# Expert weights of a streaming encoder's mixture layer: six conditional loads of 2 MB a round in place of twelve of 1 MB

## What is computed

```python
def moe(x, w_router, b_router, w_exp_gate, w_exp_up, w_exp_down):
    logits = (x @ w_router).astype(jnp.float32) + b_router.astype(jnp.float32)
    scores = jax.nn.softmax(logits, axis=-1).reshape(N, N_GROUPS, EXPERTS_PER_GROUP)
    ...
    for e in range(N_EXPERTS):
        h = jax.nn.silu(x @ w_exp_gate[e]) * (x @ w_exp_up[e])
        y = y + gates[:, e:e + 1] * (h @ w_exp_down[e])
    return y
```

## Time and profile before

| | |
|---|---|
| median of three runs | 1642.64 us (1641.89 to 1647.93) |
| profiled execution, its own time | 1645.16 us |
| span of its trace, first to last instruction | 1643.3 us |
| mean granted TensorE clock | 0.955 |
| TensorE busy (share of the span) | 1448.0 us (88%) |
| VectorE, ScalarE busy | 583.0 us (35%), 275.2 us (17%) |
| moved by DMA | 324.71 MB (millions of bytes), 198 GB/s on average |
| issues of expert loads | 6 groups of 54, 1024.0 KB each |

### The profile page before, as it was taken

One profiled execution on the slowest core, in us unless ns is written; L12 is line 12 of the kernel. 1 busy time (PEld: TensorE's weight loads), 2 busy tenths in 40 slices (PEclk: granted clock), 3 DMA queues, 4 the chain that ended last, 5 costly groups with the idle time before them and its releaser, 6 DMA issues.

```text
span 1643.3 us, 21243 instructions
## 1 busy us (share of the span) xinstructions
PE 1448.0 (88%) x6922; PEld 746.0 (45%) x6922; DVE 583.0 (35%) x1173; ACT 275.2 (17%) x671; POOL 90.4 (5%) x128
## 2 busy tenths in 40 slices
PE   4999898897899999894989999979978999867688
PEld 1588446455343433331447864555543333322234
DVE  5057674334311111014520858643361111001056
ACT  2201244201201001000121012431021100000012
POOL 2000000000000000003000000010000000000110
PEclk9999999998999999996999999989989999999889
DMA  9412111343299989997031320014434899999921
GB/s 292 158 51 94 65 52 55 129 167 132 78 337 391 365 323 370 408 409 301 1 119 52 104 106 21 32 55 152 157 119 152 295 315 359 407 407 405 339 73 55
DMA packets 156874, 324.71 MB, mean 198 GB/s; under 512 B 11548, under 2 KB 14164, under 8 KB 156796
## 3 DMA queue, kind: packets, MB, share of 16 engines
q1 hardware_dynamic: 142410, 279.56, 46.6%
q0 software_dynamic: 7104, 25.69, 4.2%
q10 hardware_dynamic: 7282, 18.49, 2.9%
HBM read 427.52 MB, written 28.32 MB: 277 GB/s over the span
## 4 chain that ended last, share of the span: by engine, by line
issue 51%; PE 33%; SPq 6%; DMA 4%; POOL 3%; DVE 2%; ACT 1%; DVEq 0%; POOLq 0%; ACTq 0%
PE psum L1226 16%; PE psum L1253 8%; PE psum L1286 4%; SPq L680 3%; SPq L679 2%; POOL rr L724 2%; DMA region<-in_w_exp_up_dram 2%; PE psum L1207 1%; SPq L667 1%; PE psum L1168 1%; PE psum L1227 1%; DMA region<-in_w_exp_down_dram 1%; ACT xT L1506 1%; POOL region L776 1%; DMA xT<-mixed_rows,seat 1%
## 5 line engine op out<-in xcount | busy, mean ns | idle before, releaser
L1226 PE MATMUL psum<-ring,xT 128*64 128x512 f32 x800 | 359.9, 602 | 35.0 <-ACT xT L1506 15.2
L1227 PE MATMUL psum<-region,xT 128*64 128x512 f32 x800 | 360.6, 603 | 0.0
L1226 PEld LDWEIGHTS psum<-ring,xT 128*64 128x64 f32 x800 | 108.1, 139 | 249.9 <-issue 249.9
L1253 PE MATMUL psum<-ring,region 128*64 128x512 f32 x400 | 178.2, 597 | 13.4 <-DMA region<-in_w_exp_down_dram 6.4
L1254 PE MATMUL psum<-region 128*64 128x512 f32 x400 | 178.4, 597 | 0.0
L879 PE MATMUL psum<-xT,ring 128*128 128x272 f32 x768 | 176.5, 393 | 0.0
L879 PEld LDWEIGHTS psum<-xT,ring 128*128 128x128 f32 x768 | 145.8, 190 | 30.1
L938 PE MATMUL psum<-ring,xT 128*128 128x512 f32 (+1 forms) x288 | 135.9, 616 | 7.2 <-DVE region L1693 7.2
L2037 DVE COPY region<-psum 128x512 f32<-128x512 f32 x25 | 17.3, 692 | 351.2 <-PE psum L1254 351.2
L1286 PE MATMUL psum<-ring,xT 128*128 128x512 f32 x256 | 117.4, 617 | 1.5 <-issue 1.5
L1253 PEld LDWEIGHTS psum<-ring,region 128*64 128x64 f32 x400 | 54.4, 138 | 122.7 <-issue 122.7
(11 more groups left out here) (266 smaller groups left out, 1535.3 us busy)
## 6 DMA issues: line engine op xcount, KB each, us to landing
region<-in_w_exp_gate_dram SPq DMA_DIRECT2D x54, 1024.0 KB
ring<-in_w_exp_gate_dram SPq DMA_DIRECT2D x54, 1024.0 KB
region<-in_w_exp_up_dram SPq DMA_DIRECT2D x54, 1024.0 KB
ring<-in_w_exp_up_dram SPq DMA_DIRECT2D x54, 1024.0 KB
ring<-in_w_exp_down_dram SPq DMA_DIRECT2D x54, 1024.0 KB
region<-in_w_exp_down_dram SPq DMA_DIRECT2D x54, 1024.0 KB
ring<-in_w_in_dram SPq DMA_DIRECT2D x24, 1024.0 KB, 8.1
expert_results<-region ACTq DMA_DIRECT2D x25, 512.0 KB, 6.2
```

The costliest lines, as they stand in the source:

```text
L1226: pe.matmul(bank[b][front, :], xeT[:, kc, front], ring[:, BLOCK_SLOT[u], kc % 4, :], start=kc == 0, stop=kc == KC - 1)
L1227: m = pe.matmul(bank[b][last, :], xeT[:, kc, last], back[:, UNIT_ROOM[u], kc % 4, :], start=kc == 0, stop=kc == KC - 1)
L1253: pe.matmul(bank[5 + n][front, :], hT[:, q, front], ring[:, BLOCK_SLOT[u], q, :], start=q == 0, stop=q == 3)
```

## The change

The two slots n = 0 and n = 1 of a matrix lie side by side in `ring` and in `back`, so one load of 2 MB can fill both. `home` gives that place and the semaphore of its first slot. The early loads (round 0, before the router is done) become one per lane and matrix as well. SP waits once per product, for the semaphore of the whole product; TensorE waits once per product, before its first step. The bytes, the flags, the slots and the order of products are as before. `gate_read` and `up_read` are still counted up by TensorE but nobody waits for them.

```diff
-                def weights(name, n, le):
+                def weights(name, le):
                     src = {"gate": wg, "up": wu, "down": wd}[name]
-                    return one(src[:, le, n, :, :])
...
+                    return src[:, le, :, :, :].rearrange("p l k c n -> p (l k) c n")
+
+                def home(name, lane):
                     if lane == 0:
...
+                        s = BLOCK_SLOT[(name, 0)]
+                        return ring[:, s:s + 2, :, :], b_full[s]
+                    s = UNIT_ROOM[(name, 0)]
+                    return back[:, s:s + 2, :, :], z_full[s]
...
-                    for n in range(2):
-                        s = BLOCK_SLOT[(name, n)]
-                        read = {"gate": (gate_read, gate_full), "up": (up_read, up_full), "down": dn_full}[name][n]
-                        hold(read, base + k + 1)
-                        e.dma_start(ring[:, s, :, :], weights(name, n, front), cond=new_front).then_inc(b_full[s], 16)
-                        e.dma_start(back[:, UNIT_ROOM[(name, n)], :, :], weights(name, n, last), cond=new_last).then_inc(z_full[s], 16)
+                    hold({"gate": gate_full, "up": up_full, "down": dn_full[1]}[name], base + k + 1)
+                    for lane, le, new in ((0, front, new_front), (1, last, new_last)):
+                        dst, done = home(name, lane)
+                        e.dma_start(dst, weights(name, le), cond=new).then_inc(done, 16)
...
                 def here(k, name, n):
 
-                    s = BLOCK_SLOT[(name, n)]
-                    pe.wait_ge(b_full[s], 16 * (base + l + k + 2))
-                    pe.wait_ge(z_full[s], 16 * (base + l + k + 2))
+                    if n == 0:
+                        pe.wait_ge(b_full[BLOCK_SLOT[(name, 0)]], 16 * (base + l + k + 2))
+                        pe.wait_ge(z_full[UNIT_ROOM[(name, 0)]], 16 * (base + l + k + 2))
```

More of the change, by code:

```diff
@@ L620, in _, with early @@
                     unit(u)
-                def weights(name, n, le):
+                def weights(name, le):
                     src = {"gate": wg, "up": wu, "down": wd}[name]
-                    return one(src[:, le, n, :, :])
-                def early(name, n, lane):
-                    s = BLOCK_SLOT[(name, n)]
+                    return src[:, le, :, :, :].rearrange("p l k c n -> p (l k) c n")
+                def home(name, lane):
                     if lane == 0:
-                        e.dma_start(ring[:, s, :, :], weights(name, n, bass.ds(l * NE, 1))).then_inc(b_full[s], 16)
-                    else:
-                        e.dma_start(back[:, UNIT_ROOM[(name, n)], :, :], weights(name, n, bass.ds(l * NE + NE - 1, 1))).then_inc(z_full[s], 16)
+                        s = BLOCK_SLOT[(name, 0)]
+                        return ring[:, s:s + 2, :, :], b_full[s]
+                    s = UNIT_ROOM[(name, 0)]
+                    return back[:, s:s + 2, :, :], z_full[s]
+                def early(name, lane):
+                    dst, done = home(name, lane)
+                    e.dma_start(dst, weights(name, bass.ds(l * NE + lane * (NE - 1), 1))).then_inc(done, 16)
                 hold(out_v, 16 * TILES * (l + 1))
@@ L638, in _ @@
                 e.dma_start(lnp1[:, 1, :], a["ln1_b"][L].to_broadcast([P, D])).then_inc(ln1p_in, 16)
-                for n in range(2):
-                    early("gate", n, 1)
+                early("gate", 1)
                 hold(soT_done, l + 1)
@@ L644, in _ @@
                 e.dma_start(prow[0:DEC, 4, :], a["p_sample"][L, 0].rearrange("l t c -> (l t) c")).then_inc(ple_in, 16)
[L645 to L648, removed]
+                early("gate", 0)
+                early("up", 1)
                 key = ("wo", 4, 0)
                 hold(full[use(key)], taken(l, key) + 1)
-                for n in range(2):
-                    early("up", n, 0)
+                early("up", 0)
                 key = ("wo", 4, 1)
                 hold(full[use(key)], taken(l, key) + 1)
-                for n in range(2):
-                    early("down", n, 0)
+                early("down", 0)
                 key = ("pp", 4, 1)
                 hold(full[use(key)], taken(l, key) + 1)
-                for n in range(2):
-                    early("down", n, 1)
+                early("down", 1)
                 hold(routed, l + 1)
@@ L674, in part_of @@
                     new_last = entry(3, k, 0, 1)
-                    for n in range(2):
-                        s = BLOCK_SLOT[(name, n)]
-                        read = {"gate": (gate_read, gate_full), "up": (up_read, up_full), "down": dn_full}[name][n]
-                        hold(read, base + k + 1)
-                        e.dma_start(ring[:, s, :, :], weights(name, n, front), cond=new_front).then_inc(b_full[s], 16)
-                        e.dma_start(back[:, UNIT_ROOM[(name, n)], :, :], weights(name, n, last), cond=new_last).then_inc(z_full[s], 16)
+                    hold({"gate": gate_full, "up": up_full, "down": dn_full[1]}[name], base + k + 1)
+                    for lane, le, new in ((0, front, new_front), (1, last, new_last)):
+                        dst, done = home(name, lane)
+                        e.dma_start(dst, weights(name, le), cond=new).then_inc(done, 16)
                 for name in ("gate", "up", "down"):
-                    for n in range(2):
-                        hold(b_full[BLOCK_SLOT[(name, n)]], 16 * (base + l + 1))
-                        hold(z_full[BLOCK_SLOT[(name, n)]], 16 * (base + l + 1))
+                    for lane in range(2):
+                        hold(home(name, lane)[1], 16 * (base + l + 1))
                     if name != "down":
```

## The result

The changed kernel took 1676.45 us as the median of four runs (1671.22 to 1679.88), the kernel before 1642.95 us beside it. The ratio is 1.0193 with a 95% interval of 1.0166 to 1.022: slower by 31.7 us (27 to 36), where 15.6 us were forecast, and outside the range of 1648 to 1666 us. The profiled execution took 1677.7 us for a span of 1675.9 us, 32.6 us more than that of before.

The account below looks back on a forecast made before the run. TensorE's products bound rounds with hidden loads, DMA bounds two back-to-back stretches, A and B. A 7.7 + B 6.8 + up(5) 1.1 = 15.6 us on 1642.64 gave 1658 us, range 1648 to 1666 us.

Parts of the forecast that it names:

- The regimes, the rate, the size of a load: Expert rounds: some hide their loads, successive both-lane rounds are DMA-bound; rate stays 405 GB/s with 2 MB loads.
- SP's fewer issues: Six issues and their register steps a round go away on SP, whose time is covered: 0 us.
- TensorE's fewer waits: The wait at the fifth step of each product goes away; products already run without a gap: 0 us.
- B: Back-to-back loads in layer 1, 152 us: 6.8 us slower from later start and whole-product wait; 5.3 without slow clock.
- A: Back-to-back loads ending layer 0, 112 us: 3.36 + 3.44 + 0.9 = 7.7 us slower, bounds 6.8 and 8.7.
- the later start: First load of a dry-queue stretch waits for the whole product, shifting all behind it: 3.36 us in layer 0.
- the slow start: Last product of layer 0 begins at the lower clock after a wait: 0 to 1.9 us, taken as 0.9.
- Both-lane products outside A and B: Isolated both-lane loads on an empty queue: 15.98 us available, 12.5 us plus start needed, still hidden by 2 us or so.
- up(5): Up product of round 5, layer 0: new wait of 2.2 us if the queue was dry; taken 1.1, bounds 0 and 2.2.
- One is tighter: Only one isolated both-lane load, up of round 5 in layer 0, has a one-lane down load queued ahead: 1.1 us.
- What follows has its weights in time: Layer 1, behind the up product of round 10: later products have their weights in time, no further cost forecast.
- the isolated rounds don't hold: Rival: nine both-lane loads in rounds 2, 5, 7 of layer 0 wait 1 us or so each: 1667 us, 10 in 100.

Follow-up runs that it names:

- the control of SP's work: Kernel before with only the table entries of a round read once for gate and up: 1646.95 us, ratio 0.9996.
- the two edits: Against the kernel before, with 1 MB loads: late release 9.7 us, whole wait 13.3 us, together 1676.6 us, ratio 1.0196.
- late release: Kernel before, still 1 MB loads and waits by halves, but both pieces of a product leave only after all of it: 1652.6 us, ratio 1.0059.
- whole wait: Kernel before, still 1 MB loads released by halves, but a product starts only when all four pieces are there: 1658.61 us, ratio 1.0081.
- the four kernels with 1 MB: Against the kernel before: late release 1.0059, whole wait 1.0081, both together 1.0196; the change with down loaded in 1 MB pieces 1.0191.
- the two with parts: Kernel before, 1 MB loads, whole release and whole waiting only for gate and up: 1670.33 us, ratio 1.0141; only for down: 1664.48 us, ratio 1.0114.

## Why the prediction was wrong

- **The regimes, the rate, the size of a load: right.** The saturated stretches keep 406 GB/s, and loads of 1 MB and 2 MB give 1.0196 and 1.0193. The rule of the Trainium skill ("DMA: Bandwidth & Descriptors", section "Anatomy of one DMA — SWDGE (gpsimd) path"), by which two loads of 1 MB would cost an estimated 2 us more than one of 2 MB, shows in no run of such queued loads. SP's fewer issues at nothing fit as well: with the change's waits, twelve loads and six give the same time, and the control of SP's work gave 0.9996. TensorE's fewer waits were not tried by themselves.
- **B, 6.8 us: right, and for the reason given.** L1 is 6.9 us longer. Counted from the layer's first turning, the last product that waits in B, up(10), starts 3.28 us later than its second half did before (1535.37 - 1278.46 for 1509.09 - 1255.46; 3.41 forecast), and the turning behind it comes 3.69 us after that (8.46 - 5.03 = 3.43 forecast).
- **A, 7.7 us, came out at 11.6.** Its two main terms are the two edits' costs alone: 3.36 us for the later start (3.6 measured with late release), 3.44 + 0.9 for the last product (4.8 with whole wait). What the sum left out is that the queue runs dry once more inside A. After the weights of gate(12) are there, TensorE runs two whole products without a wait before the memory of down is given back at 738.84, and by 739 the queue has moved the loads that were in it. The four windows from 739 to 743 moved 0.506 of the 1.62 million bytes that they hold at 405 GB/s, which is 2.75 us. Of the other 1.1 us, 0.6 are the slow start, for which 0.9 was taken: from its first to its last pair the last product takes (763.03 - 755.04) - (742.43 - 739.41) = 4.97 us more than its second half did before, where 3.44 + 0.9 were forecast. The 0.5 us left are not assigned to a row.
- **"Both-lane products outside A and B": the step that failed.** It gave a load on an empty queue 15.98 us, its price 12.5 us, and so a reserve of 2 us or so; but for up(5) these rounds were put at nothing, and they came out 8.4 us longer. The 15.98 us have both half products taken out already, and hold (TensorE came 15.78 us after the issue of down(7)); the price was too small. The load of down(7), issued at 610.75, is multiplied from 627.19 on, 16.44 us later, and TensorE waits for it. Two things make up the difference. The start is what I could not read off before: of the 1.62 million bytes that the windows from 611 to 615 hold at 405 GB/s only 0.53 moved, which is 2.7 us. And from 611 to 628 the engines moved 17 x 309 thousand = 5.25 million bytes, 4.19 of them weights, so the row traffic was 1.06 million and not the 0.52 of one gather: 1.3 us more. 12.5 + 2.7 + 1.3 is 16.5 us; the start alone would still have fitted into the 3.5 us left.
- **down(2), nothing forecast, costs 1.8 us.** "One is tighter" was wrong, there are two: gate(3) is a one-lane load queued ahead of down(2), as down(4) is ahead of up(5). From 472.92, when up is given back, 4 + 2 + 4 MB run up to down(2), which is multiplied 33.38 us later, at 506.30; TensorE came for it 1.60 us before.
- **up(5), 1.1 us (bounds 0 and 2.2), came out at 5.4.** I shifted its own last issue by 3.24 us. But the run of loads that ends with it begins when gate is given back: 4 + 2 + 4 MB from 529.72 on. At 2.59 us a piece that is 25.9 us, with 2.6 us of row traffic, 1.8 us for the start (0.3 up to 530 and 1.5 from the three windows behind it) and 0.86 for the completion 31.2; 32.8 were measured (what the 1.6 us left are is not shown; it may be more row traffic, as the run is longer than a round). Up to the moment at which TensorE came for them, 562.55 - 3.25 = 559.30, there were 29.6 us. In the kernel before, the first half of gate leaves at 523.79, which is 3.4 us earlier in its round (5.9 on the clock, less 2.5 us by which the changed kernel is late there), and only half of up(5) has to be there when its product starts: the same run fits. After the wait the clock is lower: in the window at 564 the granted clock is 0.50, which is 1.2 GHz. So the round is 5.39 us longer: the product starts 3.67 us later in it (18.59 us behind the turning at 543.96, for 14.92 us before, 3.25 of it the wait), and the turning at 572.20 comes 1.72 us later still, which is the slow start.
- **The last down of layer 1, nothing forecast, costs 2.9 us.** "What follows has its weights in time" was true by half a product only. Its one 2 MB load leaves at 1560.63 on an idle queue and is multiplied 10.15 us later.
- **The rest, 2.8 us,** is within the scatter of that column.

Of the 17.0 us between the sum and the span's 32.6, 7.3 lie in the early rounds, 3.9 in A, 2.9 in the last down, 0.1 in B and 2.8 in the rest. The rival "the isolated rounds don't hold" named the right place, with 10 chances in 100, but for a wrong reason (room in the queue for 2 MB); with 1 MB loads they fail as well. What made my reserve look safe is that each load was priced as if it stood alone: without its start, without half of the row traffic, and without the loads queued ahead of it. Each edit alone takes half a product, 3.44 us, and the isolated rounds hold against either (22.8 to 23.2 us with each); together they don't.

That the surplus appears when both half products are gone is shown by the four kernels with 1 MB; that gate and up together set up(5)'s wait, and down the last load's, by the two with parts. Gate and up were not tried apart, so that the run begins with gate's release is argued from the times of SP's issues.

## What to carry to other kernels

Cost a later release by the run of loads that hangs on it: from the moment the memory is given back on an empty queue to the last product fed by that run, all bytes in between, and (here) 2 to 3 us for the start. If a slot is given back late and also waited for whole, subtract both from the same reserve. Costs measured one by one don't add: 9.7 and 13.3 us by edit, and 23.2 and 18.8 us by matrix, both made 32. Merging loads saves the issuing engine's time and nothing else that these runs show, so look first whether that engine is late at all: here it was only when its loads were doubled.

## What was unexpected of the hardware

A load on an idle queue is slow to come up. The issues of down(7) end at 611.42 and 612.35; nothing moves before 612, and then 57, 150 and 324 GB/s in the three windows up to 615, 416 after it. For gate(5) it is 57, 186 and 350. The Trainium skill ("DMA: Bandwidth & Descriptors", section "Latency and other measured facts") gives about 0.6 us to the first byte for loads that SP issues. The rows, in which the first bytes move between 0.6 and 1.6 us after the end of the first issue, don't contradict that; but most of the 2.7 us go by after the first bytes.

An issue that finds room takes a time on SP that goes by the load's pattern rather than by its bytes: 0.37 us for 512 KB and 1 MB, 0.39 for 2 MB of gate or up, 0.65 for 2 MB of down, whose two halves of the columns lie apart in the source. A skipped load takes 0.08 us, and 0.15 in that last form.
